# Selecting experts in slices of two heads, with half of their weighted sums as diagonal products on TensorE and 16 row buffers

## The reference

```python
q = (h @ w_query).reshape(B, S, 8, 2, 128)
sc = jnp.einsum('bshcd,hckd->bshck', q, sub_keys)      # 2 x 128 sub-key scores for each of 8 heads
sv, si = lax.top_k(sc, 16)
cand_s = (sv[..., 0, :, None] + sv[..., 1, None, :])   # 256 pairs a head
cand_i = (si[..., 0, :, None] * 128 + si[..., 1, None, :])
top_s, top_j = lax.top_k(cand_s, 16)
eidx = jnp.take_along_axis(cand_i, top_j, axis=-1)     # 16 experts a head, 128 a token
gate = softmax(top_s)
u, v = expert_u[eidx], expert_v[eidx]                  # rows of 1024 floats
act = gelu(einsum('tnd,td->tn', u, h)) * gate
x = x + einsum('tn,tnd->td', act, v)
```

## Time and profile before

| | |
|---|---|
| median of 3 runs | 2093.8 us (2089.73 to 2102.74) |
| the profiled execution | 2101.64 us, span 2099.8 us |
| first gather issued, last gather issued | 1304.11 us, 2065.48 us |
| gathers | 512, each 128 rows of 4 KB |
| busy in the span | PE 1251.0 us, DVE 1248.7, POOL 589.4, ACT 324.0 |

### The profile page before, as it was taken

How to read it: one execution, slowest core, us unless ns; L and a number is a source line. 1 busy time by engine, 2 the same in 40 slices (tenths; PEclk the granted TensorE clock), 3 DMA queues, 4 the chain that set the end, 5 groups by cost and what they waited for, 6 DMA issues and landing times.

```text
span 2099.8 us, 19946 instructions
## 1 busy us (share of the span) xinstructions
PE 1251.0 (60%) x7582; PEld 1113.9 (53%) x7582; DVE 1248.7 (59%) x1837; ACT 324.0 (15%) x344; POOL 589.4 (28%) x551
## 2 busy tenths in 40 slices
PE   8899889998998899997998897000000013100003
PEld 6798889887997699887976497000000002000002
DVE  2542654104463343004785448898999999789885
ACT  1340244003420232004411111000000000000001
POOL 1000000000000000000000001878776777777662
PEclk9899999999999899998998898555555556555556
DMA  9546555347563544444422357899998999899994
GB/s 383 219 140 224 189 192 180 120 160 280 183 229 130 181 162 138 160 147 148 148 93 78 120 185 240 318 351 326 327 383 336 368 386 381 297 350 377 371 374 174
DMA packets 107161, 501.26 MB, mean 239 GB/s; under 512 B 12217, under 2 KB 12289, under 8 KB 80081
## 3 DMA queue, kind: packets, MB, share of 16 engines
q0 software_dynamic: 77296, 288.42, 36.9%
q1 hardware_dynamic: 29792, 211.83, 28.8%
HBM read 499.14 MB, written 1.06 MB: 238 GB/s over the span
## 4 chain that ended last, share of the span: by engine, by line
PE 41%; issue 15%; POOL 12%; DVE 11%; another core or an unknown queue 4%; DMA 2%; ACT 2%; DVEq 1%; SPq 0%; ACTq 0%
PE G L710 36%; POOL mod L410 6%; POOL arena L410 5%; DVE xs L1694 2%; PE G L1045 1%; DVE ybuf L1694 1%; DVE mod L1627 1%; DMA mod<-in_peer_v,mod 1%; DVE mod L1625 1%; PE T L792 1%; DMA ring<-in_wpack 1%; DVE mod L1466 1%; DVE hT L1218 1%; DVEq L1694 0%
## 5 line engine op out<-in xcount | busy, mean ns | idle before, releaser
L1136 DVE TENSOR_TENSOR wlo<-ring,whi 128x2048 fp32r<-128x2048 f32 x80 | 183.2, 2291 | 230.0 <-ACT whi L432 229.6
L710 PE MATMUL G<-ring,arena 128*128 128x256 f32 x1280 | 282.0, 384 | 7.4 <-DVE arena L1254 4.7
L710 PEld LDWEIGHTS G<-ring,arena 128*128 128x128 f32 x1280 | 246.4, 193 | 42.3 <-DVE arena L1254 5.2
L1084 PE MATMUL G<-mod 128*128 128x512 f32 x16 | 11.2, 868 | 409.8 <-issue 390.4
L1084 PEld LDWEIGHTS G<-mod 128*128 128x128 f32 x16 | 4.5, 293 | 416.9 <-issue 395.9
L410 POOL DMA_INDIRECT mod<-in_peer_u,mod x128 | 164.7, 1287 | 123.4 <-DVE mod L1665 75.8
L432 ACT ACTIVATE whi<-ring 128x2048 fp32r<-128x2048 f32 x80 | 153.0, 1913 | 287.5 <-PE G L710 251.4
L710 PE MATMUL G<-ring,cB 128*128 128x256 f32 x768 | 170.7, 383 | 9.5 <-DMA ring<-in_wpack 9.5
L1238 DVE RECIPROCAL small<-small 128x2 f32<-128x2 f32 x4 | 0.7, 166 | 286.9 <-ACT small L492 286.9
L792 PE MATMUL T<-consts,xs 128*128 128x128 f32 x32 | 5.4, 316 | 275.0 <-DVE xs L1702 272.9
L1681 DVE SCALAR_TENSOR_TENSOR arena<-arena 128x1024 f32<-128x1024 f32 x128 | 155.1, 1229 | 20.5 <-DMA arena<-in_peer_u,mod 16.5
(11 more groups left out here) (306 smaller groups left out, 2115.5 us busy)
## 6 DMA issues: line engine op xcount, KB each, us to landing
ring<-in_wpack SPq DMA_DIRECT2D x200, 1024.0 KB, 5.0
mod<-in_ada_b POOLq DMA_DIRECT2D x2, 2048.0 KB, 14.9
mod<-in_ada_b POOLq DMA_DIRECT2D x2, 1024.0 KB, 10.8
mod<-in_peer_u,mod POOLq DMA_INDIRECT x128
arena<-in_peer_u,mod POOLq DMA_INDIRECT x128
mod<-in_peer_v,mod POOLq DMA_INDIRECT x128
arena<-in_peer_v,mod POOLq DMA_INDIRECT x128
xs<-in_x SPq DMA_DIRECT2D x1, 1024.0 KB, 15.5
```

The lines of the kernel that those rows point to most:

```text
L710: ins = nc.tensor.matmul(dst, lhs(k), rhs(k), start=(first and k == 0), stop=(last and k == DC - 1))
L1136: V.tensor_tensor(wlo[:, q % 2, :], ring[:, raw % RING, :], whi[:, q % 2, :].bitcast(F32), ALU.subtract).then_inc(raw_free[raw % RING], 1)
```

## The change

- The queries of a block are made in four parts, for two heads each (a "slice"; there are 8 slices or steps in all, four for each token block), and PE makes the scores of a slice one step after its queries. psc has a part for each block.
- `choose(q)` makes the whole selection of slice q: key tops, pairs, pair tops, places, sub-keys, expert numbers.
- The gathers are issued in the order of `GATHERS`: 32 rows of u of slice q, then 32 rows of v of slice q-1, and so on. There are 16 buffers, eight of them on `late`, memory that the dense layers' split operands had; gather 12 waits for all sub-score products, since its buffer lies on pqT.
- Even rows of v are summed by DVE as before. For an odd row ACT makes a 128x128 diagonal matrix of its weights (`spread`), and PE multiplies it by the row, in two products of 128x512 that accumulate in PSUM tile M over the block (`sum_rows`). `peer_done` adds the sum in M as well.
- DVE's order in a step: 32 dots of slice q, the 16 sums of slice q-1, the weights of slice q, the selection of slice q+2. Its loops are written out. ACT makes gelus and exponentials by slices.
- The weights' load of the projection goes ahead of the gathers, PE's projection ahead of the last slice's sums of its block, and `embed_add(0)` behind the selection of the last slice.

```diff
-GBUF = 8
+GBUF = 16
+HEADS = 2
+SLICE = HEADS * PK
+SLICES = H // HEADS
+STEPS = TT * SLICES
+DIAGS = 8
...
-FEWER = {"down0": 2, "down1": 2, "b_out": 2, "att": 2, "conv": 2, "peer_q": 4, "ple": 4}
+FEWER = {"down0": 2, "down1": 2, "b_out": 2, "att": 2, "conv": 2, "ple": 4}
...
+GATHERS = [(kind, q // SLICES, q % SLICES * SLICE + n) for step in range(STEPS + 1) for kind, q in ((0, step), (1, step - 1))
+           if 0 <= q < STEPS for n in range(SLICE)]
+PLACE = {row: g for g, row in enumerate(GATHERS)}
+
+
+def by_pe(row):
+
+    return row[0] == 1 and row[2] % 2 == 1
+
+
+READ = [sum(not by_pe(row) for row in GATHERS[:g + 1]) for g in range(len(GATHERS))]
+SUMMED = [sum(by_pe(row) for row in GATHERS[:g + 1]) for g in range(len(GATHERS))]
+
+
+def row_used(row):
+
+    g = PLACE[row]
+    return ("row_summed", SUMMED[g]) if by_pe(row) else ("row_read", READ[g])
...
-        psc = carve(arena, 6144, (HC, NKEYS))
+        psc = [carve(arena, 6144, (HC, NKEYS)), carve(late, 8192, (HC, NKEYS))]
         cand = carve(arena, 8192, (H, PK, PK))
         h2 = carve(arena, 10240, (TT, D))
 
-        gbufs = [carve(modf, 0, (4, D)), carve(arena, 0, (4, D))]
+        gbufs = [carve(modf, 0, (4, D)), carve(late, 0, (4, D)), carve(late, 4096, (4, D)), carve(arena, 0, (4, D))]
+        diags = cB
...
-            for t in range(TT):
-                pool.wait_ge(sem("eidx_ready"), t + 1)
-                if t == 1:
-                    load(wproj, A["w_ple_proj"], "l_proj")
-                for kind, table in ((0, A["peer_u"]), (1, A["peer_v"])):
-                    base = (2 * t + kind) * NSEL
-                    for n in range(NSEL):
-                        if base + n == 4:
-                            pool.wait_ge(m_ready, SPARE0["psc"] + 4)
-                        pool.wait_ge(sem("row_used"), base + n + 1)
-                        j = n % GBUF
-                        nc.gpsimd.indirect_dma_start(
-                            out=gbufs[j // 4][:, j % 4, :], out_offset=None, in_=table,
-                            in_offset=bass.IndirectOffsetOnAxis(ap=eidx[:, t, n:n + 1], axis=0),
-                        ).then_inc(sem(f"row{j}"), 16)
+            load(wproj, A["w_ple_proj"], "l_proj")
+            for g, row in enumerate(GATHERS):
+                kind, t, n = row
+                if kind == 0 and n % SLICE == 0:
+                    pool.wait_ge(sem("eidx_ready"), t * SLICES + n // SLICE + 1)
+                if g == 12:
+                    pool.wait_ge(m_ready, SPARE0["psc"] + STEPS)
+                if g >= GBUF:
+                    what, count = row_used(GATHERS[g - GBUF])
+                    pool.wait_ge(sem(what), count)
+                j = g % GBUF
+                nc.gpsimd.indirect_dma_start(
+                    out=gbufs[j // 4][:, j % 4, :], out_offset=None, in_=(A["peer_u"], A["peer_v"])[kind],
+                    in_offset=bass.IndirectOffsetOnAxis(ap=eidx[:, t, n:n + 1], axis=0),
+                ).then_inc(sem(f"row{j}"), 16)
...
+            def expert_gelu(q):
+                t, s = divmod(q, SLICES)
+                act.wait_ge(sem("row_read"), READ[PLACE[0, t, (s + 1) * SLICE - 1]])
+                n = slice(s * SLICE, (s + 1) * SLICE)
+                nc.scalar.activation(actv[:, t, n], dots[:, t, n], ACT.Gelu_apprx_tanh).then_inc(sem("gelu"), 1)
+
+            def spread(q):
+
+                t, s = divmod(q, SLICES)
+                act.wait_ge(sem("weighted"), q + 1)
+                for n in range(s * SLICE + 1, (s + 1) * SLICE, 2):
+                    k = SUMMED[PLACE[1, t, n]] - 1
+                    if k >= DIAGS:
+                        act.wait_ge(sem("row_summed"), k - DIAGS + 1)
+                    nc.scalar.activation(diags[:, k % DIAGS, :], ident, ACT.Copy,
+                                         scale=actv[:, t, n:n + 1]).then_inc(sem("diag_made"), 1)
...
+            for q in range(STEPS):
+                queries(q)
+                sub_scores(q)
             gate_exp(0)
-            sub_scores(1, 0)
-            queries(1, 1)
-            sub_scores(1, 1)
+            gate_exp(1)
             expert_gelu(0)
-            gate_exp(1)
-            embed(0)
-            expert_gelu(1)
+            for q in range(1, STEPS):
+                if q + 1 < STEPS:
+                    gate_exp(q + 1)
+                expert_gelu(q)
+                spread(q - 1)
+                if q == SLICES:
+                    embed(0)
+            spread(STEPS - 1)
...
+            for q in range(STEPS):
+                b = BLOCK0["peer_q"] + q
+                block_free(b)
+                for half in range(2):
+                    h = 2 * (UNIT0["peer_q"] + q) + half
+                    w = raw(h)
+                    for c in range(2):
+                        ins = product(G[:, b % 2, 0, (2 * half + c) * P:(2 * half + c + 1) * P],
+                                      lambda k: w[:, k, c * P:(c + 1) * P],
+                                      lambda k: hT[:, k, q // SLICES * P:(q // SLICES + 1) * P])
+                    ins.then_inc(raw_free[h % RING], 1)
+                if q != 1:
+                    sub_scores(max(q - 1, 0))
+            sub_scores(STEPS - 1)
+            def sum_rows(q):
+                t, s = divmod(q, SLICES)
+                if q == SLICES:
+                    pe.wait_ge(sem("x_ready"), 5)
+                for n in range(s * SLICE + 1, (s + 1) * SLICE, 2):
+                    g = PLACE[1, t, n]
+                    k = SUMMED[g] - 1
+                    pe.wait_ge(sem(f"row{g % GBUF}"), 16 * (g // GBUF + 1))
+                    pe.wait_ge(sem("diag_made"), k + 1)
+                    for nb in range(2):
+                        ins = nc.tensor.matmul(M[:, nb, :], diags[:, k % DIAGS, :],
+                                               gbufs[g % GBUF // 4][:, g % 4, nb * 512:(nb + 1) * 512],
+                                               start=(n == 1), stop=(n == NSEL - 1))
+                    ins.then_inc(sem("row_summed"), 1)
...
+            for t in range(TT):
+                for s in range(SLICES):
+                    if s == SLICES - 1:
+                        embed_proj(t)
+                    sum_rows(t * SLICES + s)
+                embed_gate(t)
...
+            def choose(q):
+                t, s = divmod(q, SLICES)
+                h = slice(s * HEADS, (s + 1) * HEADS)
+                dve.wait_ge(m_free, SPARE0["psc"] + q + 1)
+                key_top(t, 2 * HEADS * s, 2 * HEADS)
+                pairs(HEADS * s, HEADS)
+                pair_top(HEADS * s, HEADS)
+                places(HEADS * s, HEADS)
+                sub_key(0, HEADS * s, HEADS)
+                sub_key(1, HEADS * s, HEADS)
+                V.scalar_tensor_tensor(out=eidx[:, t, s * SLICE:(s + 1) * SLICE],
+                                       in0=i12[:, 0, h, :].rearrange("p h k -> p (h k)"), scalar=float(NKEYS),
+                                       in1=i12[:, 1, h, :].rearrange("p h k -> p (h k)"),
                                        op0=ALU.mult, op1=ALU.add).then_inc(sem("eidx_ready"), 1)
+                link(V.tensor_copy(gmax[:, h], topv[:, h, 0]))
+                V.tensor_tensor(topv[:, h, :], topv[:, h, :], bcast(gmax[:, h], 2, PK), ALU.subtract).then_inc(sem("topv"), 1)
+            def row_in(row):
+                g = PLACE[row]
+                dve.wait_ge(sem(f"row{g % GBUF}"), 16 * (g // GBUF + 1))
+                return gbufs[g % GBUF // 4][:, g % 4, :]
+            def expert_dots(q, n0=0, n1=SLICE):
+                t, s = divmod(q, SLICES)
+                for n in range(s * SLICE + n0, s * SLICE + n1):
+                    row = row_in((0, t, n))
+                    V.scalar_tensor_tensor(out=row, in0=row, scalar=1.0, in1=h2[:, t, :], op0=ALU.mult, op1=ALU.mult,
+                                           accum_out=dots[:, t, n:n + 1]).then_inc(sem("row_read"), 1)
+            def expert_weights(q):
+                t, s = divmod(q, SLICES)
+                h, n = slice(s * HEADS, (s + 1) * HEADS), slice(s * SLICE, (s + 1) * SLICE)
+                dve.wait_ge(sem("gate_exp"), q + 1)
+                link(V.tensor_reduce(gsum[:, h], topv[:, h, :], AX_X, ALU.add))
+                link(V.reciprocal(grec[:, h], gsum[:, h]))
+                link(V.tensor_tensor(gateT[:, t, n].rearrange("p (h k) -> p h k", h=HEADS), topv[:, h, :],
+                                     bcast(grec[:, h], 2, PK), ALU.mult))
+                dve.wait_ge(sem("gelu"), q + 1)
+                V.tensor_tensor(actv[:, t, n], actv[:, t, n], gateT[:, t, n], ALU.mult).then_inc(sem("weighted"), 1)
+                if s == 0:
+                    link(V.memset(ybuf[:, t, :], 0.0))
+                dve.wait_ge(sem("weighted"), q + 1)
+            def expert_sums(q):
+                t, s = divmod(q, SLICES)
+                for n in range(s * SLICE, (s + 1) * SLICE, 2):
+                    row = row_in((1, t, n))
+                    if n >= 4:
```

(79 more changed lines are left out.)

137 lines of the change are left out of this document (41 added, 96 removed).

## The result

The changed kernel took 2170.0 us (median of 4 runs, 2150.7 to 2176.09) where the kernel before took 2097.35 (4 runs, 2089.73 to 2102.74) on the same chip: ratio 1.0338, 95% interval 1.0299 to 1.0377. I had forecast 2095, range 2035 to 2137; it lies outside. The profiled execution took 2176.09 us, span 2174.3. Later runs of the changed kernel gave another size of the same sign, 1.010 to 1.012. They are from chips that the record numbers 15, 1 and 8 (the other experiments add chip 7); it gives no number for the chip of the first runs, which I call the first chip, so that I can't rule out that it is one of them at another hour.

The account below looks back on a forecast made before the run. It took DVE's two-input work to throttle POOL's issuing and so the gathers. Slice 0's dots, six 100 us cycles, last steps and tail summed to 2100 in profile time, 2095 on the median's scale; eight in ten, 2035 to 2137.

Parts of the forecast that it names:

- Start: Ahead of the expert stage: first gather near 1256, 48 us sooner; gather 12 at 1303; 12 early gathers gain 16 us.
- Selection of 15.1 us a slice, POOL standing 3.6 us: DVE's one-piece selection in each step: 15.1 us, 17.2 with weights; POOL stands 3.6 us once 16 buffers are full.
- Buffers: Gather row buffers, sixteen instead of eight: POOL's stalls and the 4.02 us late-row wait should go, inside the 1.33 pace.
- Bursts: 32 dots after each selection: back to back in 36.7 us, POOL held to 1.98 us a gather, 18 gathers issued.
- Sums: Last 30 rows of each cycle: 1.33 us a row (bounds 1.28 to 1.50), 39.9 us plus 6.2 for landing.
- PE: PE's sum rows: 3.4 or 1.7 us by clock against 2.66 between rows; costed at nothing inside the cycles.
- The slower one: Rival: irregularly spaced sums hold POOL, 1.50 instead of 1.33; +59 us in full, likely 2125; decided above 1.42; chance 0.25.
- POOL slips in: Rival: in bursts every third dot may let an issue pass, DMA pace 1.28 between; -40 us, 2055; chance 0.22.
- The third, no hold: Rival: POOL issues at 1.24 us beside any dot, a cycle takes 86 us; 2005 us; chance 0.05.
- a cycle: Expert stage, one selection start to the next: 17.2 + 36.7 + 46.1 = 100 us for 64 gathers, six times.
- the whole sum: All phases from gather 12 to the tail: 2100 us in profile time against a span of 2099.8.
- the embedding's extras: DVE work counted apart from the cycles: first block's closing, zeroing and embedding, 7.8 us.

Follow-up runs that it names:

- the repeats: The changed kernel run again unchanged on chips 15, 1 and 8: 2094.22, 2086.19 and 2094.4 us, ratios 1.0122, 1.0117 and 1.0099 to the kernel before.
- a3_again: The changed kernel run again unchanged, last of three such runs on other chips: 2094.4 us, ratio 1.0099 to the kernel before.
- b0_again: The kernel before, run again unchanged on chip 1 for a second trace: 2064.3 us.
- e6_psum: The changed kernel with the dots' second input (h2) in PSUM tile T, last transposes moved to M: 1995.36 us, ratio 0.9637 to the kernel before.
- a1_again: The changed kernel run again unchanged, first of three such runs on other chips: 2094.22 us, ratio 1.0122 to the kernel before.
- b1_psum: The kernel before with the dots' second input (h2) copied to PSUM tile M: 2032.47 us, ratio 0.9818 to the kernel before.
- e8_press: The changed kernel with two 1 MB DRAM-to-DRAM copies at the start of each of six selections: 2096.0 us, ratio 1.0112 to the kernel before.
- e2_spread: The changed kernel with the selection cut into pieces between the sums, slice 2's selection moved too: 2046.16 us, ratio 0.9895 to the kernel before.
- e5_both: The changed kernel with the selection in pieces among the sums and the dots' h2 in PSUM: 1993.68 us, ratio 0.9628 to the kernel before.

## Why the prediction was wrong

- *Start.* First gather 1256 forecast, 1258.8 measured; gather 12 at 1303 (1300 to 1311), measured 1312.2 on the first chip, 1297.7 to 1302.1 in the repeats. Right but for PE's slow spell. The dots of slice 0 ended 13.7 us late on the first chip, 4.6 in a3_again.
- *Selection of 15.1 us a slice, POOL standing 3.6 us.* Right in length in every later run, 27 us three times and once 17 on the first chip: 38.9 of the 74 us missed (span 2174.3 against 2100), the largest single term. **This is the term that failed**, and the step behind it is in "Buffers": I read the 4.02 us stop of the earlier trace rows and the idle time in the earlier trace rows as rows and buffers being late and let them go away with 16 buffers. The group said "issue", and b0_again, with the same rows and the same 8 buffers, has 3.7 us of idle time there instead of 19.5; in the first trace DVE's signals, counters and branches came late. A disturbance that delays signals and instructions one by one, each by some steps of 0.70 us, costs a phase of long dots and sums little (26.6 us in the old kernel) and a string of 60 small instructions much, all the more as 16 buffers run full behind it. I had no rival for it. POOL's nine stops, 21.8 us, were no term of mine either; they lie in the sums and bursts of the first trace, and in its last two steps (8.3 and 5.8 us over forecast).
- *Bursts.* The hold in bursts is shown: issues 1.5 us and over for 10 to 17 of some 20 (mean 1.5 to 1.8 by burst, so 1.8 to 2.1 from start to start, forecast 1.98), and 0.94 once the operand is in PSUM. POOL issued 20 rows, not 18: the bursts of before, counted again (11 of five or more dots without a gap, 52 intervals), give 1.84 us and with it the 20. A held issue ends 0.81 us after the dot's end, not 0.9. Yet 32 dots took 40.3 us (a3_again, mean of six), not 36.7: in four of the six bursts DVE meets rows that are still on their way from the 27th or 28th dot on, and waits 3 to 5 us there; in e6_psum, with 27 to 29 rows issued, it never waits and a burst is 36.6 us. I had let all 32 run back to back on rows that POOL issues at half pace in the same burst: +21.4 us in six cycles, 24.4 on the first chip. This is the second step that failed, and it stands on every chip.
- *Sums.* Pace 1.33 forecast; 195 rows in 260.2 us, 1.33, in a3_again; 193 in 263.0, 1.36, on the first chip. Phases of 43.4 us instead of 46.1 paid back 16.4.
- *PE.* Clock 0.93 in the sums, 31.0 us of PE for 15 rows in 45: it keeps up. In a1_again 12 of POOL's gaps end with PE, each of the usual 0.3 us: nothing, as costed. In the first trace four of POOL's nine stops, 11 us, end with PE, but it was PE's signal that was late and not its work: rows ended at 1778.63 and 1781.07, no signal of PE is recorded between 1776.34 and 1781.95 and then five are within 0.24 us, and ACT and POOL, which wait for them, go on at 1781.98 and 1782.21.
- *Rivals.* The slower one (2125) had the right sign by a mechanism that is not there: the sums' pace stayed under its 1.42. "POOL slips in" was half right (20 rows, not 18) and worth nothing. The third, no hold, put 2005 on a kernel whose dots don't hold POOL: e6_psum took 1995 and 1999. The arithmetic held (a cycle forecast at 86, measured at 84 to 87) and the premise didn't. That premise was the inference in the Trainium skill, "SBUF — State Buffer", Who interferes with whom, that descriptor generation isn't stopped; b1_psum and e6_psum contradict it for this kernel's gathers. An issue here also reads its row numbers (eidx) from SBUF, so no run tells whether that reading or the making of the descriptors was held.
- *Size.* On the other chips the whole sum was 7 to 21 us off (2100 against 2092.8, 2086.8 and 2079.0). That it came so near was in part luck: in a3_again a cycle, the embedding's extras taken off, took 100 us as forecast because +21.4 in the dots and -16.4 in the sums nearly cancel. The change is still 1% slower there, since the kernel before loses its stalls too. The prices measured apart, around different kernels, are 1.8% for the buffers and 2.6% for PE's half on one side and 2.2% for the lump with its burst on the other. What the slices' order costs beyond, some 3.4% if the prices add up, I didn't separate.
- *Open.* What makes signals and instructions come late in the first runs, one every 0.70 us. It fell into full DMA at most places (share 1.01 to 1.03 at eight; 0.75 at 1789 to 1793 in the first trace of before), but full DMA alone doesn't bring it about (e8_press, the repeats), and it struck one engine while another worked on. No later run has such a string; e2_spread and e5_both have five single gaps of 1.4 to 1.8 us that end in "issue". Slow fetching of instructions is one rival, and the late signals and the DMA records speak against it for the selection's spell: neither of the two queues of kind "instruction" moved a packet from 1450 to 1472 (nor in PE's spell from 1266 to 1276). Another is the recording of the profile itself, as the same two traces have lost updates; all four runs of the first chip have a span from a profile, so no run tells. Whether it is that chip, its place beside other memory traffic, or the hour wasn't to be told from here.

## What to carry to other kernels

Where POOL issues gathers beside DVE work, put one input of DVE's long operations in PSUM before anything else is moved: one changed operand gave 1.8% in the old kernel and 4.4 to 4.8% in the new, where the whole reordering without it lost 1%. Work put together in one piece is free only if what follows it lets the issuing engine catch up. And where a group's idle time before its instructions says "issue" or "remote" in an engine that should have been ready, find out what it is, or run the kernel before a second time elsewhere, before forecasting that it goes away.

## What the runs showed of the hardware

- A DVE operation with two SBUF inputs holds an indirect DMA's issue on POOL (1.99 us instead of 0.94), at a DMA share of 0.21 as at full; with one SBUF and one PSUM input it doesn't (0.93 and 0.94).
- Where in the operation an issue starts decides. In a3_again 72 of 72 issues that began 0.04 to 0.12 us after a dot's start were held, 12 of 13 that began earlier went free; beside sums, issues begun up to 0.07 us after the start went free (12 of 12, and 180 of 180 in the first trace of before). An issue held from within the operation ends 0.81 us after the operation's end.
- In the first traces, DVE was idle up to 4.6 us ahead of single instructions of its selection (2.5 us in the one shown) and PE up to 1.6 ahead of single products while the core's DMA engines were full (share 1.01 to 1.03, 420 GB/s), and the instructions came closely again once they were empty. Their starts stood multiples of 0.70 us apart, on both engines and in both kernels, while other engines ran on; in the selection the signals that DVE waited for were themselves late, by 1.5 to 7.7 us for the four shown. On the four chips of the later runs the same share had no such effect, with 2 MB of DRAM copies in the same window neither. The Trainium skill, "Runtime: NRT & Kernel Launch", Instruction fetch mechanics, takes the fetching of straight-line instructions to be mostly hidden; no run here tells for certain whether it was that.
